# Decay and beta rows of a gated DeltaNet block formed from a split column, in a one-core decoder layer on Trainium2

## What is computed

```python
decay = jnp.cumsum(g, axis=-1)
gamma = jnp.exp(jnp.where(causal, decay[..., :, None] - decay[..., None, :], -jnp.inf))
k_beta = k * beta
a_low = jnp.where(strict, jnp.einsum("bhnid,bhnjd->bhnij", k_beta, k) * gamma, 0.0)
```

## Time and profile before

| | |
|---|---|
| median of 3 runs | 1817.28 us (1816.93 to 1817.96) |
| profiled execution | 1816.72 us |
| its span, first to last instruction | 1814.9 us |
| granted TensorE clock, mean | 0.999 of full speed |
| TensorE matmuls busy | 1799.1 us, 99% |
| VectorE, ScalarE, GpSimd busy | 1091.4, 859.9, 100.2 us |

### The profile page before, as it was taken

The page is one execution under the profiler, slowest core; times in us unless marked ns, Lnnn a source line. Parts: engine busy times, 40 slices in busy tenths (PEclk is TensorE's granted clock), DMA queues, the critical chain, the costliest instruction groups (busy, mean ns, idle before and its releaser), DMA issues.

```text
span 1814.9 us, 28443 instructions
## 1 busy us (share of the span) xinstructions
PE 1799.1 (99%) x10790; PEld 1469.6 (81%) x10790; DVE 1091.4 (60%) x1523; ACT 859.9 (47%) x1369; POOL 100.2 (6%) x81
## 2 busy tenths in 40 slices
PE   8999999999999999999999999999999999999998
PEld 6888787787787888888888888888888888888886
DVE  5577686767876677775555555555444455555454
ACT  6454455554644545554444444444433344444443
POOL 0021030030210000000000000000000000000100
PEclk9999999999999999999999999999999999999999
DMA  7544443444434544445656665555555555555554
GB/s 270 172 160 132 140 151 118 162 131 139 138 130 140 190 156 166 155 155 185 205 197 202 198 209 186 187 186 185 188 196 190 193 189 186 186 186 192 190 192 139
DMA packets 88121, 316.42 MB, mean 174 GB/s; under 512 B 9728, under 2 KB 10496, under 8 KB 87888
## 3 DMA queue, kind: packets, MB, share of 16 engines
q1 hardware_dynamic: 86608, 311.20, 52.0%
q0 software_dynamic: 832, 3.02, 0.4%
q10 hardware_dynamic: 576, 0.71, 0.1%
HBM read 312.79 MB, written 2.10 MB: 173 GB/s over the span
## 4 chain that ended last, share of the span: by engine, by line
PE 96%; DVE 3%; issue 1%; ACT 0%; DMA 0%; POOLq 0%; POOL 0%; ACTq 0%; DVEq 0%
PE acc L327 29%; PE acc L328 28%; PE acc L329 28%; PE J L384 1%; PE J L423 1%; DVE w_lo L1194 1%; PE J L415 1%; DVE cT L1225 1%; PE J L522 1%; PE J L574 1%; PE J L427 1%; PE J L391 1%; PE J L372 1%; PE J L536 1%; PE J L451 0%
## 5 line engine op out<-in xcount | busy, mean ns | idle before, releaser
L1194 DVE TENSOR_TENSOR w_lo<-raw,w_hi 128x1024 fp32r<-128x1024 f32 x584 | 713.5, 1227 | 514.5 <-ACT w_hi L794 513.2
L794 ACT ACTIVATE w_hi<-raw 128x1024 fp32r<-128x1024 f32 x584 | 617.7, 1063 | 645.1 <-PE acc L329 637.7
L327 PE MATMUL acc<-w_hi,hT_hi 128*128 128x512 f32 x1440 | 577.7, 401 | 0.4 <-DVE hT_lo L1212 0.4
L328 PE MATMUL acc<-w_lo,hT_hi 128*128 128x512 f32 x1440 | 562.4, 391 | 0.0
L329 PE MATMUL acc<-w_hi,hT_lo 128*128 128x512 f32 x1440 | 561.6, 390 | 0.0
L327 PEld LDWEIGHTS acc<-w_hi,hT_hi 128*128 128x128 f32 x1440 | 270.6, 188 | 64.9 <-issue 7.0
L329 PEld LDWEIGHTS acc<-w_hi,hT_lo 128*128 128x128 f32 x1440 | 270.6, 188 | 57.9
L328 PEld LDWEIGHTS acc<-w_lo,hT_hi 128*128 128x128 f32 x1440 | 270.9, 188 | 52.4 <-issue 1.0
L327 PE MATMUL acc<-w_hi,act_hi 128*128 128x512 f32 x512 | 199.3, 389 | 0.0
L329 PE MATMUL acc<-w_hi,act_lo 128*128 128x512 f32 x512 | 199.2, 389 | 0.0
L328 PE MATMUL acc<-w_lo,act_hi 128*128 128x512 f32 x512 | 199.2, 389 | 0.0
(11 more groups left out here) (234 smaller groups left out, 1346.4 us busy)
## 6 DMA issues: line engine op xcount, KB each, us to landing
raw<-weights SPq DMA_DIRECT2D x584, 512.0 KB, 3.3
xres<-x POOLq DMA_DIRECT2D x4, 512.0 KB, 6.0
xres<-x SPq DMA_DIRECT2D x3, 512.0 KB, 9.2
y<-nat SPq DMA_DIRECT2D x6, 256.0 KB, 3.7
fgain_sb<-fgain SPq DMA_DIRECT2D x1, 1024.0 KB, 5.4
masks_sb<-masks POOLq DMA_DIRECT2D x1, 576.0 KB, 7.7
xres<-x SPq DMA_DIRECT2D x2, 256.0 KB, 5.5
y<-nat ACTq DMA_DIRECT2D x2, 256.0 KB, 3.1
```

Source lines behind the costliest of these rows:

```text
L327: mm(o, aT_hi[:, kt, tok], w_hi[:, c % RING, w], start=first, stop=False)
L328: mm(o, aT_hi[:, kt, tok], w_lo[:, c % RING, w], start=False, stop=False)
L794: A(w_hi[:, slot], raw[:, slot], ACT.Copy).then_inc(hi_ready, 1)
L1194: tt(w_lo[:, slot], raw[:, slot], w_hi[:, slot].bitcast(F32), ALU.subtract).then_inc(lo_ready, 1)
```

## The change

- A group's column is split on GpSimd into a float32r part (128x8) and its rest, each is spread over the mask (128x512), and the row is the sum of two float32r matmuls with float32r ones. It holds for the decay row and for the beta row. The buffers are parts of `og_hi` and `og_lo` that are free until the last group ends.
- The decay row's matmul stands behind step 12 in place of 11.
- VectorE uses the decay row at h = 5, behind the keys' SiLU, in place of h = 4 ahead of it.

```diff
-PE_ROWS, PE_KK, PE_KQ, PE_QT, PE_OT = 11, 29, 46, 82, 124
+PE_ROWS, PE_KK, PE_KQ, PE_QT, PE_OT = 12, 29, 46, 82, 124
...
-DVE_ROWS, DVE_NK, DVE_KK, DVE_EYE, DVE_KQM, DVE_NQ, DVE_VB, DVE_Z = 4, 7, 14, 17, 18, 23, 35, 41
+DVE_ROWS, DVE_NK, DVE_KK, DVE_EYE, DVE_KQM, DVE_NQ, DVE_VB, DVE_Z = 5, 7, 14, 17, 18, 23, 35, 41
...
+        row_hi, row_lo = (a[:, 12:14, :].rearrange("p a t -> p (a t)") for a in (og_hi, og_lo))
+        chunk_r = og_hi[:, 14, 0:P]
+        col_hi, col_lo = (a[:, 15, 0:U] for a in (og_hi, og_lo))
...
+            def row_sum(out_):
+
+                mm(out_, chunk_r, row_hi, start=True, stop=False)
+                return mm(out_, chunk_r, row_lo, start=False, stop=True)
...
-                    mm(J[:, 2], chunk_ones, mat(M_B0), start=True, stop=True).then_inc(rows_done, 1)
+                    row_sum(J[:, 2]).then_inc(rows_done, 1)
...
-                    mm(J[:, 1], chunk_ones, mat(M_B0), start=True, stop=True)
+                    row_sum(J[:, 1])
...
+            def rows_of(col, mask, n):
+
+                tt(col_hi, col, ones[:, 0:U], ALU.mult).then_inc(col_link, 1)
+                pool.wait_ge(col_link, 2 * n + 1)
+                tt(col_lo, col, col_hi.bitcast(F32), ALU.subtract)
+                tt(row_hi.rearrange("p (u c) -> p u c", u=U), wide(col_hi.bitcast(F32), C), over(mask, U), ALU.mult).then_inc(col_link, 1)
+                pool.wait_ge(col_link, 2 * n + 2)
+                tt(row_lo.rearrange("p (u c) -> p u c", u=U), wide(col_lo.bitcast(F32), C), over(mask, U), ALU.mult).then_inc(rows_rhs, 1)
+
+            pool.wait_ge(params_in, 48)
+            ts(chunk_r, chunk_ones, 1.0, None, ALU.mult)
...
-                tt(mat(M_B0), wide(scu(G), C), over(tri64, U), ALU.mult).then_inc(rows_rhs, 1)
+                rows_of(scu(G), tri64, 2 * g)
...
-                tt(mat(M_B0), wide(scu(BETA), C), over(eye64, U), ALU.mult).then_inc(rows_rhs, 1)
+                rows_of(scu(BETA), eye64, 2 * g + 1)
```

More of the change, by code:

```diff
@@ L263, in hybrid_trunk @@
         nq_done = sem("nq_done")
+        col_link = sem("col_link")
         rows_rhs, rows_done, arg_done, exp_done, mask_done = (
```

## The result

The changed kernel took 1827.05 us (median of 6 runs, 1826.82 to 1829.3) against 1817.26 us (6 runs, 1816.87 to 1817.96) for the kernel before: ratio 1.0053, 95% interval 1.0043 to 1.0064. It is 9.8 us slower. The profiled execution spans 1824.8 us against 1814.9.

The account below looks back on a forecast made before the run. It took TensorE, busy 99% of the span at full clock, as the bound. 9.3 us lost at the queries' turn less 1.6 kept gave 7.7 over 1816.72, with the median 0.56 above: 1824.9 us, range 1820.4 to 1828.2.

Parts of the forecast that it names:

- The row matmuls: On TensorE, two float32r matmuls take 0.46 us where one row matmul cost 0.87: gain 0.41 each, 8 times.
- The bound on which they gain nothing: The two float32r matmuls of a row do not keep their neighbours' pace and gain nothing.
- The row's use behind the SiLU: On VectorE, the later row use delays the exponentials and the product behind the queries' turn: 1.51 us three times, 1.35 once.
- The port: GpSimd's second large decay product runs between two VectorE w_lo and makes the second w_lo 0.86 us late.
- the two bounds: For the w_lo delay: 0 if VectorE keeps the port through both w_lo, some 1.3 us if the small products are slow.
- rival 1: VectorE keeps the port, so only the order of SiLU and row's use counts: 4.2 us slower, 1821.5; chance 0.20.
- The sum: 9.3 us lost at the queries' turn, 1.6 kept at the beta row: 7.7 us slower, forecast 1824.9 us.
- rival 2: GpSimd's small products or float32r writes slower, row matmuls gaining nothing, or beta row late: 1826.5 to 1828.5; chance 0.10.
- Rival 3: No wait at the queries' turn, so the matmuls' gain shows: 2.6 us faster, 1814.7, or 1813.0; chance 0.10.

Follow-up runs that it names:

- early_par: Changed kernel with columns copied earlier, decay row's matmul behind step 11, its use at h = 4, both step-17 turns at step 18: 1814.94 us against 1817.87 before.
- beta_only: Kernel before with only the beta row formed by the split column, decay row and VectorE's order as before: 1817.07 us against 1817.87.
- order_only: Kernel before with only VectorE's use of the decay row moved to h = 5, behind the keys' SiLU: 1824.01 us, ratio 1.0034.
- port_late: Changed kernel with GpSimd's second decay product also waiting until VectorE has done both w_lo: 1822.67 us, ratio 1.0024 to the kernel before.
- filler: Changed kernel with unread float32r matmuls, 4 ahead of the keys' turn and 6 ahead of the queries' turn: 1825.89 us, ratio 1.0042 to before.
- after_again: The changed kernel run once more, unaltered, to see whether the granted clock falls again: 1827.28 us, ratio 1.005 to the kernel before.

## Why the prediction was right, and where it was short

**The row matmuls: right.** In early_par L451 to L452 to the next product is 0.23 each, in all four windows; the third:

```profile
357.39 0.39 PE L451 MATMUL J<-og_hi 128*128 128x512 f32 x1
357.62 0.39 PE L452 MATMUL J<-og_lo,og_hi 128*128 128x512 f32 x1
357.84 0.39 PE L332 MATMUL acc<-w_hi,hT_hi 128*128 128x512 f32 x1
```

In three windows of the changed kernel the first of them takes 0.34, since its weight load had waited 0.3 us for GpSimd's product; the wait for the SiLU behind it hides that. beta_only gives 0.42 a window against 0.41 forecast. The bound on which they gain nothing is out.

**The row's use behind the SiLU: right, and the largest term.** order_only has it alone: 6.1 us in the windows, 5.9 forecast. VectorE stood idle for 1.13 us ahead of the SiLU, waiting for the tanh, and TensorE 1.6 us ahead of the queries' turn in three windows and 1.25 in the first. The step that made this readable was to ask what filled the gap between tap and SiLU before the change.

**The port: right, in kind and size.** The choice between the two bounds was the one that hung on 0.04 us, the forecast against rival 1. GpSimd got the port between the two `w_lo` in all four windows of each kernel that had this clash: its product 2.07 long against 2.1 forecast, the `w_lo` 2.06 against 2.1. port_late, which takes the clash away and keeps all the rest, is 0.8 a window faster, where the term was 0.86. The reason given for the choice was the 0.04 us; every product came 0.04 to 0.06 us behind the start of the first `w_lo`, and no run moved it, so whether those 0.04 us or the waiting itself decided is not shown. The Trainium skill ("SBUF — State Buffer", Who interferes with whom) calls the shared port pair an exclusive lock and lets the order of issue decide who blocks. These rows agree: the product waited since 360.92 and came ahead of the `w_lo` that would have started at 362.01. Of two back to back with a third in wait the Trainium skill says nothing.

**The sum: 2.1 us short of the measured 9.8.** (Its terms add to 1824.96 us; the 1824.9 written is a rounding too low.) The measured 1827.05 us lies outside the forecast's own range, 1823.5 to 1826, and inside that of rival 2, 1826.5 to 1828.5. By the time alone rival 2 would have won, and it is luck that the range stated for the whole, made wide for that rival, covers a loss from another cause. The windows at full clock add to 1.89 + 3 x 1.99 = 7.9 us, against 7.7 forecast, and 0.4 lies ahead of them. The rest, 1.6 us, is a term that I did not have at all: the granted clock. I had taken it as full because it was full before, where the longest wait in these windows for what the change touches was 0.5 us, in the weight queue. The premise at the head of the prediction, a clock at the full level, so that a microsecond lost on TensorE is one of the whole, is what failed: behind two stops close together the clock fell to 1.2 GHz for most of 3.7 us in one window of each profile, 1.6 us on top. filler, whose matmuls fill the stops to 0.2 us, takes the 1.6 away, and after_again shows the fall at another window. I also named only the queries' turn as a wait of the changed kernel and hid the keys' in it; for the time that made no difference, for the clock the two stops came together: order_only has the 1.6 us stop alone, and its profile shows no fall (its windows agree within 0.15). With one window of four falling in the changed kernel, one such profile does not show that it takes both stops.

**The rivals.** Rival 1 would have been right with another arbitration (port_late, 4.7 us more than before, 4.2 forecast). Of rival 2 nothing came, though the time lies in its range: the decay row's small products took 0.20 each, the large ones 1.04 in float32r as in float32. For the beta row the first small product came behind a `w_lo` and took 1.12; the row's operand was ready 1.2 us before TensorE came in the second window (1.4 forecast), and there was no wait. Rival 3 needed the chain to be 1.5 us shorter than its links, and each link came as long as its row.

## What to carry to other kernels

Before moving work off a critical chain, look at what it stands in front of: here it filled a gap in which the next instruction waited for another engine anyway, so that moving it behind gained 0.2 us for one reader and cost 1.5 at the turn of the other. Adding work to an idle engine is free only where it shares nothing with the engine on the chain; place it beside instructions that read PSUM, not between two that read two SBUF buffers. And when a change brings TensorE to a stop, read the granted clock of the stretch behind it, since a stop can cost more than it lasts.

## What the runs showed of the hardware

- GpSimd with an SBUF read waiting takes the port between two back-to-back VectorE instructions of two SBUF inputs, though VectorE's second starts 0.09 us before the first has ended in the usual case: products of 1.04 us became 2.07, the second `w_lo` of 1.22 became 2.06, in all four windows of five kernels.
- TensorE's granted clock fell to 1.2 GHz behind stops of 1.0 and 1.6 us that were 1.1 us apart (0.54 over 3.7 us, matmuls 0.43 apart in place of 0.23), in one of four windows with much the same stops, and in another one in the next profile. With matmuls that nobody reads in the stops it stayed at 2.4 GHz in the one profile taken.
- A product of GpSimd that writes float32r takes the 1.04 us of one that writes float32.
